# Loading the compression's weights one stage earlier, and spreading the row copies over the sparse attention

## The chip, the cores and the metric

The kernel runs on one core of one Trainium2 chip. The metric is the device time of one execution in microseconds; lower is better. TensorE multiplies matrices (PE; its weight loads are PEld), VectorE (DVE) and ScalarE (ACT) do elementwise work, GpSimd (POOL) a little of it, and SyncE (SP) issues most of the transfers. SP, ACT and POOL each have a DMA queue of their own (q1, q10 and q0 in the profile); all three are served by the same 16 DMA engines.

## The reference, cut to what matters

The program is one inference step of a two-layer decoder trunk: a prompt of 256 tokens and 8 samples of 8 new tokens each. Layer 0 is dilated attention beside a convolution module; layer 1 is a sparse attention with three branches (compressed, selected, sliding window). Of layer 1 this matters here:

```
def compress(x, pos, w1, b1, w2):          # once for keys, once for values
    blocks = concat(chunk[i], chunk[i+1]) + pos          # 32 rows, step 16
    h = silu(einsum('bnlgd,lde->bnge', blocks, w1) + b1)
    return einsum('bnge,ed->bngd', h, w2)

rows     = stack([kc, vc, ks, vs])         # new rows of this step
cs_full  = concat([cache_c_kv paged by page_table, rows])
win_full = concat([win_hist, stack([kw, vw])])
# outputs: rows of prompt and samples, and the last 512 rows of win_full for each
```

Each sample has 2048 past rows, in 16 pages of 128 rows; which page is read from `page_table`. The compression reads a page's raw keys and values, the selected branch its other two rows. `w1` is 2 x 32 x 128 x 128 floats (4 MB).

## The kernel before, in words

The program is a row of stages, each a block of code with a stream of instructions for every engine, and a barrier of all engines between one stage and the next. Engines wait for each other only on semaphores. The stages around the change:

- `block_even_out_odd_in`: the output projection of layer 0 (`out`), then the input projection of layer 1 (`proj`, from here on "the odd projection"). `proj` makes 11 groups of 512 output rows. Each group's weights come as four quarters of 1 MB on SP's queue into four buffers; a quarter's buffer is loaded again when PE has finished with it. ACT casts a quarter (`w_hi`, L352), DVE makes the remainder (`w_lo`, L414), PE multiplies (`zc`, L318 and L324). POOL's queue carries, after each group, one 4 MB piece of a cache copy from HBM to HBM (`send`, L1389), once the load of the gate (`mix<-z`, L1403), and at the end the store of the gate (L1405). SP stores the residual `xT` to `xt` after its last weights (L1334).
- `block_sample_c`: the sparse attention of the 8 samples. SP loads the page table (L1683), then for each sample 16 pages of raw rows (`raw`, 256 KB each, L1699) and 16 pages of the selected branch (`sel`, L1712). For each page SP first reads the page number from on-chip memory into a register (L1687). `raw` is one buffer in four pieces of four pages; a piece is loaded again when PE has turned its rows. POOL loads the tables of the bias (`bias_sc`, `gt`), fills the queries of sample 0, and issues the copies of rows to the outputs. ACT issues the compression's weights (`cmp_w`, `cmp_pos`, `cmp_b`, L1576 to L1582) and then evacuates.
- PE in this stage runs a software pipeline over samples (`body`): `turn_raw` transposes two pages, `taps` multiplies the turned rows with `w1`. `body(b)` does the attention of sample b, the second half of the compression of sample b+1, and, from its step 16 of 32 on, the first turns of sample b+2. `body(-1)` has no attention: steps 0 to 15 finish the turns of sample 0 and do its key taps, steps 16 to 31 turn the first rows of sample 1 between the value taps of sample 0. So `body(-1)` stops at its step 16 until the first piece of sample 1's raw rows is there.
- `pos_products` multiplies the positions with `w1` (64 small products), `sum_parts` adds them up to a bias that the first hidden layer needs.

SP's instructions run in order, and what SP does in this stage before it can issue sample 1's raw rows is written out as

```
load_raw(0, True)
for i in range(4): ...   # qs, then kn, ov, hs
load_rest(0, True)
load_raw(1)
```

Of the kernel before, what the change touches and what calls it, by code (L numbers as in the profile page):

```python
# [12 lines left out]
ALU = mybir.AluOpType  # L13
# [1282 lines left out]

def block_even_out_odd_in(nc, k):

    with k.scope():  # L1300
        mixed = Mix(k, "2")
        mix, gate = mixed.mix, mixed.gate
        xT = k.sb("xT2", [P, KT, T])
        gcol = k.sb("gcol2", [P, KT])
        wg, wgl = k.sb_and_lo("wg", [P, KT, P])
# [19 lines left out]
        with nc.Block() as block:  # L1325
            @block.sync
            def _(sp):
                view = lambda a: a.rearrange("(k p) t -> p k t", p=P)
# [10 lines left out]
                sp.wait_ge(xt_stored, 16)  # L1339
                sp.wait_ge(proj.z_stored, 16 * 12)  # L1340
                sp.wait_ge(proj.rows_stored, 32 * 4)
# [38 lines left out]
            @block.gpsimd  # L1380
            def _(pool):
                pool.memset(wg[:, :, :], 0.0).then_inc(wg_set, 1)
                pool.wait_ge(mixed.loaded[3], 32)
                pool.dma_start(xT[:, :, :], k.xt.rearrange("(k p) t -> p k t", p=P)).then_inc(x_in, 16)
                pieces = k.cache_pieces[15:23] + k.cache_pieces[40:46]
                link = Chain(pool, x.chain)

                def send(n):
                    pool.dma_start(*pieces[n]).then_inc(copied, 16)  # L1389

                for g in range(4):
# [15 lines left out]
                pool.wait_ge(copied, 16 * len(pieces))  # L1407

# [151 lines left out]
class Compress:  # L1560

    def __init__(self, k):
        self.k = k
        self.w1, self.w2, self.pos, self.b1, self.bias, self.nbias = (
            k.sb(name, shape, lasting=True) for name, shape in (
                ("cmp_w1", [P, 2, CB, HD]), ("cmp_w2", [P, 2, HD]), ("cmp_pos", [P, 2 * CB]), ("cmp_b1", [P, 2]),
                ("cmp_bias", [P, 2]), ("cmp_nbias", [P, 2])))
        self.parts = k.sb("cmp_parts", [P, 2 * HD])  # L1570
        self.zero = k.sb("cmp_zero", [P, 2 * HD])
        self.loaded, self.small, self.zeroed, self.done, self.parts_ready, self.summed, self.ready = (
            k.sem(n) for n in ("cmp_in", "cmp_small_in", "cmp_zeroed", "cmp_pos_done", "cmp_parts_ready", "cmp_summed", "cmp_bias_ready"))

    def load(self, act):
        act.dma_start(self.pos[:, :], self.k.cmp_pos).then_inc(self.small, 16)  # L1576
        act.dma_start(self.b1[:, :], self.k.cmp_b1).then_inc(self.small, 16)
        for i in range(2):
            for part in range(2):
                l = slice(part * CB // 2, (part + 1) * CB // 2)  # L1580
                act.dma_start(self.w1[:, i, l, :], self.k.cmp_w1[i][l].rearrange("l d e -> d l e")).then_inc(self.loaded, 16)
        act.dma_start(self.w2[:, :, :], self.k.cmp_w2.rearrange("a e d -> e a d")).then_inc(self.small, 16)  # L1582

    def pos_products(self, pe, bank, i):

        if i == 0:
            pe.wait_ge(self.small, 48)
            pe.wait_ge(self.zeroed, 1)
            pe.matmul(bank[:, 0:2 * HD], self.zero[:, 0:P], self.zero[:, :], start=True, stop=True)
        for l in range(CB):  # L1590
            o = 32 * (l % 4)
            ins = pe.matmul(bank[o:o + 1, i * HD:(i + 1) * HD], self.pos[:, i * CB + l:i * CB + l + 1], self.w1[:, i, l, :],
                            start=(l < 4), stop=(l >= CB - 4))
        ins.then_inc(self.done, 1)

    def sum_parts(self, pe, bank):
        pe.wait_ge(self.parts_ready, 1)
        for i in range(2):
            ins = pe.matmul(bank[:, 2 * HD + i:2 * HD + i + 1], self.parts[:, i * HD:(i + 1) * HD], self.k.ones[:, 0:1], start=True, stop=True)
        ins.then_inc(self.summed, 1)  # L1600

    def dve(self, dve, bank):
        dve.wait_ge(self.done, 2)
        dve.tensor_copy(self.parts[:, :], bank[:, 0:2 * HD]).then_inc(self.parts_ready, 1)
        dve.wait_ge(self.summed, 1)
        link = Chain(dve, self.ready)
        link(dve.tensor_tensor(self.bias[:, :], bank[:, 2 * HD:2 * HD + 2], self.b1[:, :], ALU.add))
        link(dve.tensor_scalar(self.nbias[:, :], self.bias[:, :], -1.0, None, ALU.mult))

def block_sample_c(nc, k):
# [3 lines left out]
    with k.scope():  # L1615
        k.compress = cmp = Compress(k)
        ptab = k.sb("ptab", [1, NB * NPG], mybir.dt.int32)
# [40 lines left out]
        pt_in = k.sem("pt_in")  # L1658
# [21 lines left out]
        with nc.Block() as block:  # L1680
            @block.sync
            def _(sp):
                sp.dma_start(ptab[:, :], dram_ap(k.page_table, 0, [(NB * NPG, 1), (1, NB * NPG)])).then_inc(pt_in, 16)  # L1683
                sp.wait_ge(pt_in, 16)

                def pages_of(b):
                    return [sp.value_load(ptab[0:1, bass.ds(b * NPG + pg, 1)], min_val=0, max_val=k.cache_c_kv.shape[0] - 1)  # L1687
                            for pg in range(NPG)]

                def load_raw(b, first=False):  # L1690
                    page = pages_of(b)
                    for pg in range(NPG):
                        n = pg * NPIECE // NPG
                        if not first and pg % (NPG // NPIECE) == 0:
                            sp.wait_ge(raw_turned, b * NR + (NRK - NR + 2 * n + 2))
                            settle(sp, k)

                        rows = k.cache_c_kv[bass.ds(page[pg], 1)].rearrange("a (n l) c g d -> (a l) n (c g d)", l=CS)[:, :, 0:2 * CKV]
                        sp.dma_start(raw[:, pg, :], rows).then_inc(raw_in[n], 16)  # L1699
# [36 lines left out]
            def _(pool):  # L1736
# [22 lines left out]
                n = 0  # L1759
                for dst, c0, c1 in ((k.out_rows_p, 0, 4 * CKV), (k.out_win_p, 4 * CKV, 6 * CKV)):  # L1760
                    pool.dma_start(dst.rearrange("t c g d -> t (c g d)"), k.kv2[0:NP, c0:c1]).then_inc(rows_out, 16)
                    n += 1
                pool.dma_start(k.out_rows_s.rearrange("b t c g d -> (b t) (c g d)"), k.kv2[NP:T, 0:4 * CKV]).then_inc(rows_out, 16)
                n += 1
                for b in range(NB):
                    pool.dma_start(k.out_win_s[b, 0:WIN - NQ].rearrange("t c g d -> t (c g d)"), k.cache_c_win[b, NQ:WIN].rearrange("t c g d -> t (c g d)")).then_inc(rows_out, 16)
                    pool.dma_start(k.out_win_s[b, WIN - NQ:WIN].rearrange("t c g d -> t (c g d)"), k.kv2[NP + b * NQ:NP + (b + 1) * NQ, 4 * CKV:]).then_inc(rows_out, 16)
                    n += 2
                with pool.Fori(1, NB) as b:
                    fill_q(b)  # L1770
                pool.wait_ge(rows_out, 16 * n)
# [17 lines left out]
            def _(act):  # L1789
                cmp.load(act)  # L1790

# [55 lines left out]
            def _(pe):  # L1847
# [143 lines left out]
                def body(b, attend=True, make=True, ahead=True, first=False):  # L1991
                    for n in range(STEPS):
                        if make:
# [5 lines left out]
                            if not attend and n == 8:  # L1999
                                cmp.pos_products(pe, ob, 1)  # L2000
                            if not attend and n == 12:
# [14 lines left out]

                for j in range(NRK):
# [376 lines left out]
class Kit:  # L2394
# [15 lines left out]

    def sb_and_lo(self, name, shape):
# [130 lines left out]
```

## Time and profile before

| | |
|---|---|
| median of three runs | 2876.9 us (2875.43 to 2877.23) |
| the profiled execution's own time | 2879.94 us |
| its span, first to last instruction | 2878.1 us |
| mean granted TensorE clock | 0.896 of 2.4 GHz |
| the odd projection's last product | 1921 us from the span's start |
| first instructions of the sparse attention of the samples | 1945.0 us |
| its end (the store of its output) | 2533 us |

Times in the views are counted from the start of the span. The profiled execution is 3.0 us above the median and 1.8 us above its own span; a change in a stage is a change of all three by the same amount.

### The profile page before, as it was taken

To read this page: it belongs to the slowest core of one execution; us is meant where nothing else is said; L and a number is where in the kernel's file an instruction comes from. 1 tells how busy PE (TensorE), PEld (TensorE's weight loads), DVE (VectorE), ACT (ScalarE), POOL (GpSimd) and SP (SyncE) were. 2 spreads that over 40 slices of the span, in tenths; PEclk is the share of its full clock that TensorE was granted. 3 is DMA by queue.
4 is the path that set the end of the run, shared out by engine and by line. 5 is a ranking of instruction groups with operands and counts; after the bars stand their busy time and mean duration, and the time that the engine had idled before them with its cause. 6 is when DMAs were issued, how large, how long until landed. Compare 5 with 4: busy or idle time off the path is not lost. (4 is left out here: it accounts for less than half of the span.)

```text
span 2878.1 us, 49626 instructions
## 1 busy us (share of the span) xinstructions
PE 2411.9 (84%) x18820; PEld 2140.5 (74%) x18820; DVE 1270.3 (44%) x2311; ACT 752.2 (26%) x1100; POOL 184.1 (6%) x326
## 2 busy tenths in 40 slices
PE   6799999899689559995679999962599999877597
PEld 3799999888589436664569999962488888666496
DVE  2436699635166123332344536720043334426545
ACT  1333333333043112220133322211133333213321
POOL 1000100000000310000023200002100000000000
PEclk8899999999899779995579999985799999958799
DMA  4787888865678799994388688888745454225382
GB/s 133 271 325 282 298 322 323 289 205 165 239 249 315 248 374 380 405 349 152 97 287 283 223 306 315 323 307 164 258 147 161 146 187 149 74 67 183 135 321 76
DMA packets 260279, 686.04 MB, mean 238 GB/s; under 512 B 31814, under 2 KB 83823, under 8 KB 256557
## 3 DMA queue, kind: packets, MB, share of 16 engines
q1 hardware_dynamic: 213790, 415.74, 41.9%
q0 software_dynamic: 17312, 229.03, 21.9%
q10 hardware_dynamic: 29072, 39.82, 4.2%
q8 instruction: 71, 1.16, 0.2%
q14 instruction: 34, 0.28, 0.0%
HBM read 631.32 MB, written 250.80 MB: 306 GB/s over the span
## 5 line engine op out<-in xcount | busy, mean ns | idle before, releaser
L414 DVE TENSOR_TENSOR w_lo<-w,w_hi 128x2048 fp32r<-128x2048 f32 x180 | 415.1, 2313 | 346.5 <-ACT w_hi L352 333.4
L352 ACT CAST w_hi<-w 128x2048 fp32r<-128x2048 f32 x176 | 335.4, 1908 | 791.8 <-DMA w<-in_w_in_even 220.9
L318 PE MATMUL zb<-xh,w_hi 128*128 128x320 f32 x1664 | 496.8, 312 | 33.0 <-ACT w_hi L348 20.6
L318 PE MATMUL zb<-xT_lo,w_hi 128*128 128x320 f32 x1664 | 494.4, 311 | 0.0
L318 PEld LDWEIGHTS zb<-xh,w_hi 128*128 128x128 f32 x1664 | 316.9, 190 | 34.5 <-ACT w_hi L348 20.7
L318 PEld LDWEIGHTS zb<-xT_lo,w_hi 128*128 128x128 f32 x1664 | 316.4, 190 | 0.2
L324 PE MATMUL zb<-xh,w_lo 128*128 128x320 f32 x1664 | 267.5, 313 | 15.5 <-DVE w_lo L414 15.5
L324 PEld LDWEIGHTS zb<-xh,w_lo 128*128 128x128 f32 x1664 | 254.0, 192 | 16.6 <-DVE w_lo L414 16.6
L1865 PE MATMUL hb<-xtc,cmp_w 128*128 128x254 f32 x1024 | 252.8, 384 | 0.0
L318 PE MATMUL zc<-xh,w_hi 128*128 128x320 f32 x704 | 208.9, 311 | 8.0 <-ACT w_hi L352 6.6
L318 PE MATMUL zc<-xl,w_hi 128*128 128x320 f32 x704 | 208.3, 310 | 0.0
L1865 PEld LDWEIGHTS hb<-xtc,cmp_w 128*128 128x128 f32 x1024 | 182.9, 192 | 21.8 <-issue 4.5
L970 PE MATMUL kps<-ident,ka 128*128 128x128 f32 x832 | 141.0, 296 | 43.1 <-DMA ka<-in_cache_a_kv 41.8
L1855 PE MATMUL xrb<-ident,raw 128*128 128x128 f32 x512 | 82.2, 286 | 110.9 <-DMA raw<-in_cache_c_kv 104.4
L1855 PEld LDWEIGHTS xrb<-ident,raw 128*128 128x128 f32 x512 | 65.8, 147 | 127.9 <-DMA raw<-in_cache_c_kv 64.7
L970 PEld LDWEIGHTS kps<-ident,ka 128*128 128x128 f32 x832 | 92.2, 146 | 87.8 <-DMA ka<-in_cache_a_kv 44.1
L1797 ACT COPY xtc<-xrb 128x512 f32<-128x512 f32 x128 | 74.9, 585 | 288.9 <-PE xrb L1855 288.9
L947 DVE COPY ktt<-kps 128x512 f32<-128x512 f32 x104 | 71.9, 692 | 167.0 <-PE kps L970 167.0
L318 PEld LDWEIGHTS zc<-xh,w_hi 128*128 128x128 f32 x704 | 133.1, 189 | 8.7 <-issue 5.4
L318 PEld LDWEIGHTS zc<-xl,w_hi 128*128 128x128 f32 x704 | 133.0, 189 | 0.1
L947 ACT COPY ktt<-kps 128x512 f32<-128x512 f32 x104 | 60.9, 586 | 226.5 <-PE kps L970 226.5
L324 PE MATMUL zc<-xh,w_lo 128*128 128x320 f32 x704 | 111.9, 312 | 3.3 <-DVE w_lo L414 3.3
(372 smaller groups left out, 3424.5 us busy)
## 6 DMA issues: line engine op xcount, KB each, us to landing
out<-in_cache_a_kv POOLq DMA_DIRECT2D x32, 4080.0 KB, 16.5
w<-in_w_in_even SPq DMA_DIRECT2D x104, 1024.0 KB, 7.5
ka<-in_cache_a_kv SPq DMA_DIRECT2D x24, 2048.0 KB, 13.1
va<-in_cache_a_kv SPq DMA_DIRECT2D x24, 2048.0 KB, 15.0
w<-in_w_in_odd SPq DMA_DIRECT2D x44, 1024.0 KB, 10.1
raw<-in_cache_c_kv SPq DMA_DIRECT2D x128, 256.0 KB, 4.0
sel<-in_cache_c_kv SPq DMA_DIRECT2D x128, 256.0 KB, 5.5
out<-in_cache_a_kv POOLq DMA_DIRECT2D x8, 4032.0 KB, 21.6
```

The source lines that it names most:

```text
L318: ins = pe.matmul(self.banks[c][:, 0:T], self.hi[:, q % 2, j, c * P:(c + 1) * P], x[:, q * self.kq + j, :], start=(q == 0 and j == 0 and m ...
L324: ins = pe.matmul(self.banks[c][:, 0:T], self.lo[:, q, j, c * P:(c + 1) * P], self.xh[:, q * self.kq + j, :], start=False, stop=(q == self ...
L352: act.copy(self.hi[:, q % 2, :, :], self.wt[:, q % 4, :, :]).then_inc(self.hi_ready, 1)
L414: dve.tensor_tensor(self.lo[:, q, :, :], self.wt[:, q, :, :], self.hi[:, q % 2, :, :], ALU.subtract).then_inc(self.lo_ready, 1)
L947: copy(ktt[:, q % 2, :], kps[q % 2][:, :]).then_inc(sem, 1)
L970: ins = pe.transpose(kps[q % 2][:, j * P:(j + 1) * P], kt[g][:, r, h * HD:(h + 1) * HD], k.ident[:, :])
L1797: act.copy(xt[:, 2 * kv:2 * kv + 2, :, chunks:chunks + 2 * n].rearrange("p g l (u n) -> p u (g l) n", n=n), xr[:, :].rearrange("p (u c n) ...
L1855: ins = pe.transpose(xr[:, (2 * u + g) * P:(2 * u + g + 1) * P], raw[:, 2 * (j % NRK) + u, (2 * kv + g) * P:(2 * kv + g + 1) * P], k.ident ...
L1865: ins = pe.matmul(hb[i][:, 0:CG * NCS], cmp.w1[:, i, l, :], xt[:, 2 * i:2 * i + 2, l % CS, l // CS:l // CS + NCS], start=(l == 0), stop=(l ...
```

## The change

Three things are done.

1. The compression's weights, positions, biases and the page table are loaded in the stage before, on POOL's queue. Their tiles lie at the addresses of `xT2` and `wg`, which are used up by then (`sb_shared` gives an address back at once, so that later tiles may lie there too). For that `xT` is stored earlier, on POOL's queue too, right after the sums of squares; the small tensors follow it, and the four parts of `w1` (1 MB each, in rows of 512 bytes) go ahead of the pieces 5 to 8.
2. SP begins the sparse attention with the raw rows: it reads a page's number and issues that page's load, sixteen times. The products with the positions stand first on PE.
3. POOL's copies of rows to the outputs go later. Those of a sample's window follow its query fill, inside POOL's loop over samples; the others follow that loop.

```
@@ block_even_out_odd_in
+        xT, wg = k.sb_shared(("xT2", [P, KT, T], F32), ("wg", [P, KT, P], F32))
+        k.compress = cmp = Compress(k)
...
             def _(sp):
...
                 proj.sync(sp)
-                sp.dma_start(view(k.xt), xT[:, :, :]).then_inc(xt_stored, 16)
...
             def _(pool):
...
+                pool.dma_start(k.xt.rearrange("(k p) t -> p k t", p=P), xT[:, :, :]).then_inc(xt_stored, 16)
+                cmp.load_small(pool)
                 for n in range(3, len(pieces)):
                     pool.wait_ge(proj.tile_done, 4 * (n - 3) + 8)
+                    if n == 5:
+                        pool.wait_ge(xt_stored, 16)
+                        pool.wait_ge(x.summed, 1)
+                        pool.wait_ge(x.ready, KT)
+                        pool.wait_ge(gl_done, 1)
+                    if 5 <= n < 9:
+                        cmp.load(pool, n - 5)
                     send(n)
@@ Compress
+    def load_small(self, eng):
+        eng.dma_start(self.ptab[:, :], dram_ap(self.k.page_table, 0, [(NB * NPG, 1), (1, NB * NPG)])).then_inc(self.small, 16)
...
+    def load(self, eng, part):
+        i, l = part // 2, slice(part % 2 * CB // 2, (part % 2 + 1) * CB // 2)
+        eng.dma_start(self.w1[:, i, l, :], self.k.cmp_w1[i][l].rearrange("l d e -> d l e")).then_inc(self.loaded, 16)
@@ block_sample_c
             def _(sp):
-                sp.dma_start(ptab[:, :], dram_ap(k.page_table, 0, [(NB * NPG, 1), (1, NB * NPG)])).then_inc(pt_in, 16)
-                sp.wait_ge(pt_in, 16)
...
                 def load_raw(b, first=False):
-                    page = pages_of(b)
+                    page = None if first else pages_of(b)
...
             def _(pool):
...
                 fill_q(0)
-                for b in range(NB):
-                    pool.dma_start(k.out_win_s[b, 0:WIN - NQ]...
+                with pool.Fori(1, NB) as b:
+                    fill_q(b)
+                    rows_of(b)
+                rows_of(0)
...
             def _(act):
-                cmp.load(act)
...
             def _(pe):
...
+                for i in range(2):
+                    cmp.pos_products(pe, ob, i)
                 for j in range(NRK):
                     turn_raw(0, j)
-                pe.wait_ge(cmp.loaded, 64)
-                cmp.pos_products(pe, ob, 0)
                 body(-1, attend=False)
```

On POOL in the odd projection, after the last sum of squares (`sq`, `sum`), there stood before: the pieces of the cache copy (`out<-in_cache_a_kv`) and the load of the gate (`mix<-z`).

```order
L1274 TENSOR_TENSOR sum<-sum,sq 128x320
L1389 DMA out<-in_cache_a_kv 64x16320 x3
L1403 DMA mix<-z 128x16x320
L1389 DMA out<-in_cache_a_kv 64x16320 x8
L1405 DMA gate<-mix 128x16x320
```

And now, at the same place:

```order
+L1454 DMA xt<-xT 128x16x320
+L1311 DMA ptab<-in_page_table 1x16x8
+L1312 DMA cmp_pos<-in_cmp_pos 128x64
+L1313 DMA cmp_b<-in_cmp_b 128x2
+L1314 DMA cmp_w<-in_cmp_w 128x2x128
+L1446 DMA out<-in_cache_a_kv 64x16320 x2
+L1318 DMA cmp_w<-in_cmp_w 128x16x128
+L1446 DMA out<-in_cache_a_kv 64x16320
+L1469 DMA mix<-z 128x16x320
+L1318 DMA cmp_w<-in_cmp_w 128x16x128
+L1446 DMA out<-in_cache_a_kv 64x16320
+L1318 DMA cmp_w<-in_cmp_w 128x16x128
```

The store of `xT` and the small tensors stand ahead of the first two of these pieces, and a part of `w1` stands ahead of each of the next pieces (the fourth follows in the same way); the load of the gate keeps its place behind piece 5.

On SP at the start of the sparse attention there stood before the load of the page table, then sixteen times the read of a page's number, then sixteen loads (the first of each are shown):

```order
-L1683 DMA ptab<-in_page_table 1x128
-L1687 TENSOR_LOAD ptab
-L1687 ISA x2
...
-L1699 ISA
-L1699 DMA raw<-in_cache_c_kv 128x1x512
...
-L1720 DMA qsc<-z 128x4x64 x4
```

And now read and load alternate from the stage's first instruction on, sixteen times:

```order
L1700 TENSOR_LOAD ptab
L1700 ISA x2
L1714 ISA
L1714 DMA raw<-in_cache_c_kv 128x1x512
...
L1735 DMA qsc<-z 128x4x64 x4
```

On PE at the same place there stood the turns of the first eight pairs of pages (`xrb`), half of the products with the positions, and the first taps (`hb`), with the other half of the products further on:

```order
L1855 MATMUL xrb<-ident,raw 128x128 x32
L1589 MATMUL ob<-cmp_zero 128x256
L1592 MATMUL ob<-cmp_w,cmp_pos 1x128 x32
L1865 MATMUL hb<-xtc,cmp_w 128x254 x2
```

And now all products with the positions come first:

```order
L1333 MATMUL ob<-cmp_zero 128x256
L1336 MATMUL ob<-cmp_w,cmp_pos 1x128 x64
L1870 MATMUL xrb<-ident,raw 128x128 x32
L1880 MATMUL hb<-xtc,cmp_w 128x254 x2
```

## Rows read from the trace of the kernel before

**Rows 1.** The page: PE's busy share in 40 slices of 72 us.

```profile
PE   6799999899689559995679999962599999877597
```

**Rows 2.** Stretches around the stage's start: length, busy of PE, PEld, DVE, ACT, POOL; clock; DMA.

```profile
1919.10:1945.00 25.90, 1.52 (x12) 1.26 (x12) 0.22 (x1) 1.54 (x3) 1.67 (x2) 0.64 0.85 313
1945.00:1985.40 40.40, 0.00 (x0) 0.00 (x0) 0.00 (x0) 1.37 (x4) 19.71 (x40) 0.50 1.02 168
1985.40:2007.60 22.20, 13.14 (x98) 8.41 (x98) 0.00 (x0) 4.68 (x8) 0.00 (x0) 0.50 0.61 174
2007.60:2028.90 21.30, 21.22 (x172) 18.11 (x168) 1.74 (x5) 5.15 (x9) 2.94 (x8) 0.99 0.73 256
2028.90:2063.70 34.80, 0.00 (x0) 0.00 (x0) 2.22 (x2) 0.00 (x0) 7.27 (x15) 0.55 1.00 344
...
2212.00:2270.00 58.00, 57.61 (x449) 46.88 (x448) 22.77 (x53) 18.16 (x38) 0.56 (x3) 1.00 0.49 163
```

**Rows 3.** Waits of PE from 1921 to 2064: total us, times, longest.

```profile
PE xrb L1855 <- DMA raw<-in_cache_c_kv: 104.4, 3, 64.5
```

**Rows 4.** Timeline of SP's queue from 1940 to 2130: start, length, count.

```profile
1945.03 0.27 SPq L1683 DMA_DIRECT2D ptab<-in_page_table  x1
1955.97 31.82 SPq L1699 DMA_DIRECT2D raw<-in_cache_c_kv  x16
1987.85 9.05 SPq L1720 DMA_DIRECT2D qsc<-z  x4
...
1999.65 1.08 SPq L1724 DMA_DIRECT2D hs<-in_c_hsum  x1
2009.73 0.37 SPq L1705 DMA_DIRECT2D win<-in_cache_c_win  x1
...
2019.87 0.29 SPq L1716 DMA_DIRECT2D vnc<-kv  x1
2029.45 87.68 SPq L1699 DMA_DIRECT2D raw<-in_cache_c_kv  x32
```

**Rows 5.** The same queue, from 1955 to 1962.7 only.

```profile
1955.97 6.57 SPq L1699 DMA_DIRECT2D raw<-in_cache_c_kv  x9
```

**Rows 6.** Landing of raw pages issued in 1940 to 1990, 2029 to 2045, 2063 to 2545.

```profile
DMA to landing us min/median/max: 19.4/27.0/31.9
...
DMA to landing us min/median/max: 29.9/30.5/31.9
...
DMA to landing us min/median/max: 3.3/3.9/5.4
```

**Rows 7.** DMA from 2026 to 2064: a queue's MB and share; issues, median landing.

```profile
q0 software_dynamic: 1008, 10.23, 76.6%
...
out<-in_cache_c_win POOLq DMA_DIRECT2D x8, 1008.0 KB, 17.3
```

**Rows 8.** Timeline of PE from 1984 to 2010, one turn of two pages.

```profile
1995.07 1.12 PE L1855 MATMUL xrb<-ident,raw 128*128 128x128 f32 x4 [0.68 <-ACT xtc L1797]
```

**Rows 9.** DMA from 1948 to 1956, ACT's queue (the parts of w1).

```profile
q10 hardware_dynamic: 707, 1.42, 83.7%
```

**Rows 10.** Stretches of the odd projection, one group each from 1708 on.

```profile
1597.00:1612.30 15.30, 15.18 (x102) 15.02 (x103) 6.18 (x6) 4.24 (x3) 0.06 (x1) 1.00 0.44 138
...
1708.00:1737.00 29.00, 25.59 (x164) 25.06 (x162) 11.84 (x9) 4.13 (x3) 1.77 (x3) 0.94 0.88 309
1737.00:1774.00 37.00, 30.49 (x196) 30.26 (x197) 22.81 (x23) 13.78 (x6) 0.45 (x2) 0.95 0.80 296
1774.00:1802.20 28.20, 28.20 (x194) 28.20 (x194) 22.45 (x21) 7.64 (x4) 0.54 (x2) 1.00 0.88 320
```

**Rows 11.** Waits of all engines from 1708 to 1775.

```profile
ACT w_hi L352 <- DMA w<-in_w_in_odd: 27.0, 3, 15.9
...
PE zc L318 <- ACT w_hi L352: 6.6, 2, 3.5
```

**Rows 12.** Waits of SP's queue from 2063 to 2545.

```profile
SPq L139 <- PE xrb L1855: 83.6, 19, 13.9
```

More of the change, by code:

```diff
@@ L1294, in make_lo, with __init__, start, pos_products @@
                                  ALU.mult, ALU.subtract).then_inc(self.ready, 1)
+class Compress:
+    def __init__(self, k):
+        self.k = k
+        self.w1, self.w2, self.pos, self.b1, self.bias, self.nbias = (
+            k.sb(name, shape, lasting=True) for name, shape in (
+                ("cmp_w1", [P, 2, CB, HD]), ("cmp_w2", [P, 2, HD]), ("cmp_pos", [P, 2 * CB]), ("cmp_b1", [P, 2]),
+                ("cmp_bias", [P, 2]), ("cmp_nbias", [P, 2])))
+        self.ptab = k.sb("ptab", [1, NB * NPG], mybir.dt.int32, lasting=True)
+        self.loaded, self.small = (k.sem(n) for n in ("cmp_in", "cmp_small_in"))
+    def load_small(self, eng):
+        eng.dma_start(self.ptab[:, :], dram_ap(self.k.page_table, 0, [(NB * NPG, 1), (1, NB * NPG)])).then_inc(self.small, 16)
+        eng.dma_start(self.pos[:, :], self.k.cmp_pos).then_inc(self.small, 16)
+        eng.dma_start(self.b1[:, :], self.k.cmp_b1).then_inc(self.small, 16)
+        eng.dma_start(self.w2[:, :, :], self.k.cmp_w2.rearrange("a e d -> e a d")).then_inc(self.small, 16)
+    def load(self, eng, part):
+        i, l = part // 2, slice(part % 2 * CB // 2, (part % 2 + 1) * CB // 2)
+        eng.dma_start(self.w1[:, i, l, :], self.k.cmp_w1[i][l].rearrange("l d e -> d l e")).then_inc(self.loaded, 16)
+    def start(self):
+        k = self.k
+        self.parts = k.sb("cmp_parts", [P, 2 * HD])
+        self.zero = k.sb("cmp_zero", [P, 2 * HD])
+        self.zeroed, self.done, self.parts_ready, self.summed, self.ready = (
+            k.sem(n) for n in ("cmp_zeroed", "cmp_pos_done", "cmp_parts_ready", "cmp_summed", "cmp_bias_ready"))
+    def pos_products(self, pe, bank, i):
+        if i == 0:
+            pe.wait_ge(self.zeroed, 1)
+            pe.matmul(bank[:, 0:2 * HD], self.zero[:, 0:P], self.zero[:, :], start=True, stop=True)
+        for l in range(CB):
+            o = 32 * (l % 4)
+            ins = pe.matmul(bank[o:o + 1, i * HD:(i + 1) * HD], self.pos[:, i * CB + l:i * CB + l + 1], self.w1[:, i, l, :],
+                            start=(l < 4), stop=(l >= CB - 4))
+        ins.then_inc(self.done, 1)
+    def sum_parts(self, pe, bank):
+        pe.wait_ge(self.parts_ready, 1)
+        for i in range(2):
+            ins = pe.matmul(bank[:, 2 * HD + i:2 * HD + i + 1], self.parts[:, i * HD:(i + 1) * HD], self.k.ones[:, 0:1], start=True, stop=True)
+        ins.then_inc(self.summed, 1)
+    def dve(self, dve, bank):
+        dve.wait_ge(self.done, 2)
+        dve.tensor_copy(self.parts[:, :], bank[:, 0:2 * HD]).then_inc(self.parts_ready, 1)
+        dve.wait_ge(self.summed, 1)
+        link = Chain(dve, self.ready)
+        link(dve.tensor_tensor(self.bias[:, :], bank[:, 2 * HD:2 * HD + 2], self.b1[:, :], ALU.add))
+        link(dve.tensor_scalar(self.nbias[:, :], self.bias[:, :], -1.0, None, ALU.mult))
@@ L1407, in _ @@
                 pool.wait_ge(copied, 16 * len(pieces))
+                pool.wait_ge(cmp.small, 64)
+                pool.wait_ge(cmp.loaded, 64)
             @block.tensor
@@ L1557 @@
 NSC = O_C + NCS
[L1560 to L1608, printed above, removed]
@@ L1611, in block_sample_c @@
 def block_sample_c(nc, k):
     with k.scope():
-        k.compress = cmp = Compress(k)
-        ptab = k.sb("ptab", [1, NB * NPG], mybir.dt.int32)
+        cmp = k.compress
+        cmp.start()
         raw = k.sb("raw", [P, NPG, 2 * CKV])
@@ L1682, in _, with page_of @@
             def _(sp):
[L1683 to L1684 removed]
+                def page_of(b, pg):
+                    return sp.value_load(cmp.ptab[0:1, bass.ds(b * NPG + pg, 1)], min_val=0, max_val=k.cache_c_kv.shape[0] - 1)
                 def pages_of(b):
[L1687 to L1688 removed]
+                    return [page_of(b, pg) for pg in range(NPG)]
                 def load_raw(b, first=False):
[L1691 removed]
+                    page = None if first else pages_of(b)
                     for pg in range(NPG):
@@ L1696, in load_raw @@
                             settle(sp, k)
-                        rows = k.cache_c_kv[bass.ds(page[pg], 1)].rearrange("a (n l) c g d -> (a l) n (c g d)", l=CS)[:, :, 0:2 * CKV]
+                        rows = k.cache_c_kv[bass.ds(page_of(b, pg) if first else page[pg], 1)].rearrange("a (n l) c g d -> (a l) n (c g d)", l=CS)[:, :, 0:2 * CKV]
                         sp.dma_start(raw[:, pg, :], rows).then_inc(raw_in[n], 16)
@@ L1998, in body @@
                                 turn_raw(b + 2, n // 2 - NRK)
-                            if not attend and n == 8:
-                                cmp.pos_products(pe, ob, 1)
-                            if not attend and n == 12:
+                            if not attend and n == 2:
                                 cmp.sum_parts(pe, ob)
@@ L2015, in body @@
                             turn(b, TURNS_AT[n])
+                for i in range(2):
+                    cmp.pos_products(pe, ob, i)
                 for j in range(NRK):
                     turn_raw(0, j)
-                pe.wait_ge(cmp.loaded, 64)
-                cmp.pos_products(pe, ob, 0)
                 body(-1, attend=False)
@@ L2409, in sb, with sb_shared @@
         return self.stacks[0 if lasting else -1].enter_context(self.nc.sbuf_tensor(name, shape, dt))
+    def sb_shared(self, *named):
+        with ExitStack() as stack:
+            return [stack.enter_context(self.nc.sbuf_tensor(name, shape, dt)) for name, shape, dt in named]
     def sb_and_lo(self, name, shape):
```

21 lines of the change are left out of this document (7 added, 14 removed).

## The prediction

> **What bounds the kernel now.** I began with the page's slices [rows 1]. PE is busy nine tenths of most of them, but slices 28 and 29 (1943 to 2087 us) show 2 and 5: the longest hole of the program, at the start of the samples' sparse attention, where the change works. Cut into stretches [rows 2], it is two holes. From 1945.0 to 1985.4 PE does nothing; from 2028.9 to 2063.7 again nothing; between them lies work of body(-1). Both end with the same releaser [rows 3]: PE waits for raw pages, 104.4 us in three waits (the longest, 64.5, counts from PE's last work before the barrier). After that it is PE that binds: 57.6 of 58.0 us in a stretch as long as one sample, the last of [rows 2]. So what counts is when PE passes the second hole; whatever makes that earlier moves all later work by as much.
>
> Who is late at the holes is read from SP's queue [rows 4]. The stage begins at 1945.03 with the page table. The first raw load goes out at 1955.97, after 10.9 us of waiting for the table and reading sixteen numbers. Nine loads go out at 0.73 us each [rows 5], then the queue backs up, and sixteen take 31.8 us. Their landing takes 27 us where an undisturbed page takes 3.9 [rows 6], since all 16 DMA engines are taken: 1.02 of their time, at only 168 GB/s [rows 2]. Most of that is w1 on ACT's queue [rows 9]. Then SP goes on in order: queries and constants until 2000.7, sixteen numbers until 2009.7, window and selected pages until 2020.2, sixteen numbers until 2029.45, and only then sample 1's raw rows. These land after another 30 us [rows 6], because POOL's row copies have 76.6% of the DMA engines' time from 2026 on [rows 7].
>
> **The second hole after the change.** It ends when sample 1's fourth raw page has landed. Counted from the stage's start:
>
> - Sixteen times a number and a load. A number costs 0.56 us (2000.73 to 2009.73 for sixteen [rows 4]), a load 0.73: 20.7 us. DMA no longer has w1 to serve, so I let the queue not back up.
> - Queries and constants: 12.9 us before [rows 4], with the backlog of raw rows ahead of them. The bound below is 6, eight issues at the 0.73 us of a load that does not back up; I take 10, in the middle.
> - Sixteen numbers 9.0; window, selected pages and new values 10.4; sixteen numbers 9.3 [rows 4]. Nothing in the change touches these.
> - Three more issues, 2.2 us, and a landing of 3.9, the later samples' [rows 6]. The row copies are gone from here, and selected pages issued before have 9.3 us to land.
>
> The sum is 65.5 us. Before, PE went on at 2063.7, which is 118.7 after the start. The difference is **53.2 us**.
>
> Is PE itself there by then? Its last raw page of sample 0 is issued 20 us after the start and lands by 24 to 28; two turns of 1.8 us remain (1.12 busy and 0.68 idle [rows 8]); steps 0 to 15 took 21.3 us [rows 2], with half of the position products in them, which now lie in the first hole. At half clock for a few us (0.50 granted, that is 1.2 GHz, after the first hole [rows 2]) this may be 3 more. So PE is at step 16 after 49 to 56 us and still waits 10 to 16 for SP. The hole shrinks from 34.8 us but does not close; SP's chain ends it, and DMA speed at the start matters only if it is worse by over 10 us.
>
> **What is added in the stage before.** Four parts of w1 go through POOL's queue beside the odd projection's weights, and that stage has little DMA left: 0.88 of the time in an undisturbed group of 28.2 us, the last of [rows 10], so 3.4 us free. A part's price comes from the queue of before: 1.42 MB at 83.7% of 8 us [rows 9] is 4.7 us per MB, so 4.9 for a part of 1.05. That is 1.5 us too much in such a group. Two of the parts fall into the stretch 1708 to 1774, where PE already waits: the load of the gate and the pieces delay the weights, ACT waits 27.0 us for them, PE 6.6 for ACT [rows 11], and the clock's share falls to 0.94 and 0.95 [rows 10]. There I count half of the two parts, 5 us at most. The bounds are 0 (the weights' four buffers take it all) and 20 (all four parts exposed). I take **5**, nearer to the lower end, because PE is busy for the whole of the group beside 0.88 of DMA time. If it is more, PE stands before ACT's next cast, and DVE and POOL's next piece stand behind PE.
>
> The Trainium skill speaks on this price too. Its page "DMA: Bandwidth & Descriptors", section Specifications, puts line rate at transfers of at least 512 bytes and the fabric's ceiling at 435 GB/s; w1 comes in rows of 512 bytes. By that a part would take 2.4 us (an estimate from that page), no group would overrun, and the time would be 2824. The row of before disagrees: with 83.7% of the engines w1 got 212 GB/s per full engine set.
>
> The earlier store of xT (2.6 MB) meets a stretch with DMA at 0.44, the first of [rows 10], so nearly 9 us of DMA time are free before the next piece; nothing, at worst inside the 20 above. POOL's new waits at piece 5 are for work done groups earlier; behind them stand the piece and the gate's load, which waits longer anyhow. The barrier's own 24 us (1921 to 1945) keep their cause, the last piece and the gate's store ahead of the last rows; nothing changes there.
>
> **The copies inside the sample loop.** One window copy of 1 MB per sample costs 2.9 us of DMA time (76.6% of 38 us for 10.23 MB [rows 7]), and DMA is half idle there (0.49 [rows 2]). SP has 12 us per sample in which it waits for PE (83.6 over seven [rows 12]), so a load delayed by a copy is still early. Cost 0; without that cover up to 2.9 per sample, 20 in all. What POOL does after its loop has the last sample's time as cover.
>
> **Sum.** From the profiled execution's 2879.94: minus 53.2, plus 5, is 2831.7; the median of the runs lies 3.0 lower, so **2829**.
>
> **Rivals.**
>
> - *The odd projection becomes DMA-bound.* For it: 0.88, and PE's waits between 1708 and 1774. Against it: the four buffers, and that groups with the same 0.88 show no wait. Price 20 instead of 5: 2844. Chance 0.15.
> - *SP's chain stays late*, since sixteen raw loads back up behind the bias tables, which stay on POOL's queue; the change then does only its second half. SP would issue sample 1 near 2029 as before and its piece would land in 6 us instead of 34: a gain of 28, minus 5: 2854. Against it: of the 1.02 in the first hole most was w1. Chance 0.08.
> - *Everything at its better end*: constants in 6 us, landing 3.3, no price in the odd projection: 57.8 us gained, 2819. Chance 0.12.
> - *Slower than before.* The copies in the loop, with their large packets, hold selected pages back past what PE needs, in each sample. It decides only from 7 us per sample on (seven times 7 is the 48 of the forecast), against a price of 2.9 and 12 us of slack. 2880 and more. Chance 0.02.
>
> The forecast itself, 2822 to 2837, has 0.61; some 0.02 remain for no visible change.
>
> **How the numbers follow.** A measurement of this kernel tells 0.2%, 5.8 us, from no change. All but the last case are far below: faster 0.96, same 0.02, slower 0.02. The range leaves out these two and the late chain, 12 in 100, and some of what spread the cases at its ends have of their own: 2815 to 2852.
>
> **What would show it.** In the changed profile, SP's first raw load stands within 1 us of the stage's start and the sixteenth some 21 us later; PE's first turn comes some 10 us after the start; the second hole is 8 to 18 us long and ends 63 to 70 us after the start, its releaser still the raw rows; their landing is near 4 us. In the odd projection the groups with a part are 0 to 5 us longer, all of it before w_hi. The forecast is wrong if SP's sixteen loads still take 30 us, if those four groups grow by 20 in all, or if a sample takes over 60 us.

## The result and the profile after

The changed kernel took 2841.06 us, the median of four runs (2838.27 to 2852.85), against 2876.16 us (2862.84 to 2877.23) for the kernel before on the same chip: a ratio of 0.9896 (95% interval 0.9856 to 0.9936). It is faster by 35 us, and 12 us above the forecast of 2829. The profiled execution is the longest of the four, 2852.85 us, with a span of 2851.3 us, 26.8 us below that of before. How that comes about, stage by stage (after minus before, from starts and ends in the two traces): up to the fourth piece of GpSimd's cache copy in the odd projection (n = 3 in the code, which counts from 0) -1.4; from there to its last product +12.4; the barrier behind it +1.2; the sparse attention of the samples -42.4; the prompt's attention +3.4. The sum is -26.8. The prediction had two terms, +5 and -53.2. Both point the right way, and both are 7 to 11 us too good.

**The sparse attention's start.** The page's PE slices first:

```profile
PE   6799999989879559995669997992899999876597
```

Where [rows 1] had a 2 and a 5 side by side there is one 2 now, from 1925 to 1996 us (the barrier and the first hole), and an 8 behind it. The stretches that answer to [rows 2], with raw(0) and raw(1) for the raw rows of samples 0 and 1: the position products and a wait, the turns of raw(0), steps 0 to 15, the second hole, and one sample's length:

```profile
1957.30:1970.30 13.00, 5.89 (x131) 3.97 (x131) 0.42 (x1) 0.00 (x0) 12.86 (x27) 0.76 0.86 158
1970.30:2000.40 30.10, 8.87 (x33) 5.72 (x33) 0.00 (x0) 4.69 (x8) 6.96 (x14) 0.50 0.82 141
2000.40:2021.30 20.90, 20.90 (x104) 18.09 (x104) 1.02 (x3) 5.15 (x9) 0.56 (x3) 0.88 0.65 240
2021.30:2033.80 12.50, 0.43 (x3) 0.08 (x2) 2.52 (x3) 0.01 (x1) 0.00 (x0) 0.68 0.44 133
2182.00:2240.00 58.00, 57.60 (x450) 46.87 (x449) 22.78 (x53) 18.12 (x38) 1.60 (x5) 1.00 0.55 181
```

PE's waits from 1921 to 2064, the line that answers to [rows 3]:

```profile
PE xrb L1870 <- DMA raw<-in_cache_c_kv: 36.0, 4, 13.6
```

104.4 us have become 36.0. The releaser is the same. SP's queue, which [rows 4] showed of before:

```profile
1958.26 20.90 SPq L1714 DMA_DIRECT2D raw<-in_cache_c_kv  x16
1979.20 14.63 SPq L1735 DMA_DIRECT2D qsc<-z  x4
1993.87 2.60 SPq L1737 DMA_DIRECT2D knc<-z  x2
...
1996.95 0.68 SPq L1739 DMA_DIRECT2D hs<-in_c_hsum  x1
2006.60 0.37 SPq L1720 DMA_DIRECT2D win<-in_cache_c_win  x1
2007.17 9.98 SPq L1727 DMA_DIRECT2D sel<-in_cache_c_kv  x16
...
2017.62 0.30 SPq L1731 DMA_DIRECT2D vnc<-kv  x1
2027.21 11.68 SPq L1714 DMA_DIRECT2D raw<-in_cache_c_kv  x16
```

Read it as a sum, from the stage's start at 1957.28: raw(0) with its numbers to 21.9, queries and constants 18.4, numbers 9.0, window and selected pages 11.3, numbers 9.3, then 6.5 to PE's first turn of raw(1) at 76.5. The row that stands out is the queries': four loads in 14.63 us, where sixteen raw loads with their numbers took 20.90. DMA from 1957 to 1982 (a queue's packets, MB, share; issues and their median landing) shows what stands there:

```profile
q1 hardware_dynamic: 1566, 2.87, 70.0%
q0 software_dynamic: 1026, 1.00, 24.3%
...
raw<-in_cache_c_kv SPq DMA_DIRECT2D x16, 256.0 KB, 8.6
bias_sc<-tab_hc POOLq DMA_DIRECT2D x16, 64.2 KB, 6.5
```

raw(0) lands in 8.6 us, not 27.0 [rows 6], but not in 3.9 either: GpSimd's queue (q0) is loading the bias tables.

**The odd projection.** Four groups of it, from one of GpSimd's pieces to the next, n = 5 to n = 9; the third answers to 1737 to 1774 in [rows 10]:

```profile
1675.50:1713.50 38.00, 34.67 (x237) 34.41 (x236) 18.20 (x13) 13.11 (x8) 2.85 (x4) 1.00 0.91 312
1713.50:1735.30 21.80, 21.80 (x150) 21.55 (x149) 6.15 (x9) 4.10 (x3) 1.64 (x2) 1.00 1.09 407
1735.30:1786.20 50.90, 31.37 (x197) 31.14 (x196) 22.81 (x21) 11.81 (x5) 1.74 (x3) 0.80 0.69 240
1786.20:1813.20 27.00, 27.00 (x187) 27.00 (x186) 21.15 (x20) 7.65 (x4) 0.56 (x2) 1.00 1.01 363
```

And the waits in the middle two, beside [rows 11]:

```profile
ACT w_hi L352 <- DMA w<-in_w_in_odd: 28.3, 3, 19.4
...
PE zc L318 <- ACT w_hi L352: 19.5, 1, 19.5
```

In the group with part 1 and piece 6, DMA is taken whole (1.09) and PE does not stop once. The price falls due one group later: PE waits 19.5 us for a cast that waits for a quarter of w, and the group takes 50.9 us in place of 37.0. The last group, with part 3, is as short as ever, at a DMA share of 1.01.

**The copies in the loop.** The wait that gives SP its slack, from 2034 to 2515 [rows 12]:

```profile
SPq L139 <- PE xrb L1870: 78.1, 19, 9.0
```

78.1 us are left of 83.6; PE's busy time in the last of the stretches above is 57.60 of 58.00, and GpSimd's copies of a sample's keys follow each other by 58.4 to 58.8 us in both traces.

### The profile page after: what moved, and what is told of

It reads as the page before. It is cut to its first block and busy times, and to the rows that moved or that the text cites. A ratio compares the mean times of both kernels' runs of the same rounds, so it can differ in the third digit from the quotient of the medians.

```text
span 2851.3 us, 49669 instructions
## 1 busy us (share of the span) xinstructions
PE 2405.1 (84%) x18820; PEld 2134.2 (75%) x18820; DVE 1270.0 (45%) x2311; ACT 751.5 (26%) x1096; POOL 193.2 (7%) x335
## 3 DMA queue, kind: packets, MB, share of 16 engines
q1 hardware_dynamic: 211724, 413.12, 42.4%
## 5 line engine op out<-in xcount | busy, mean ns | idle before, releaser
L318 PE MATMUL zb<-xh,w_hi 128*128 128x320 f32 x1664 | 496.4, 311 | 34.4 <-ACT w_hi L348 20.6
L318 PEld LDWEIGHTS zb<-xh,w_hi 128*128 128x128 f32 x1664 | 316.9, 190 | 35.9 <-ACT w_hi L348 20.7
L318 PE MATMUL zc<-xh,w_hi 128*128 128x320 f32 x704 | 209.7, 312 | 20.9 <-ACT w_hi L352 19.5
L970 PEld LDWEIGHTS kps<-ident,ka 128*128 128x128 f32 x832 | 91.6, 145 | 89.4 <-DMA ka<-in_cache_a_kv 46.1
## 6 DMA issues: line engine op xcount, KB each, us to landing
ka<-in_cache_a_kv SPq DMA_DIRECT2D x24, 2048.0 KB, 13.5
```

Source lines behind the costliest of these rows:

```text
L318: ins = pe.matmul(self.banks[c][:, 0:T], self.hi[:, q % 2, j, c * P:(c + 1) * P], x[:, q * self.kq + j, :], start=(q == 0 and j == 0 and m ...
L970: ins = pe.transpose(kps[q % 2][:, j * P:(j + 1) * P], kt[g][:, r, h * HD:(h + 1) * HD], k.ident[:, :])
```

## The experiments

Ten kernels ran in three jobs, each beside the kernel before (medians 2870.82, 2876.42 and 2871.12). The table has the times, and three readings of each profile: the third group of the odd projection (n = 7 to n = 8), TensorE's first turn of raw(1), and GpSimd's second copy of keys (knb), from which on every sample takes the same time. The last two count from the sparse attention's start.

| kernel | median us (lowest to highest, runs) | ratio to before, 95% | group | raw(1) | knb |
|---|---|---|---|---|---|
| before | 2876.16 (2862.84 to 2877.23, 4) | | 37.0 | 118.7 | 165.4 |
| the change | 2841.06 (2838.27 to 2852.85, 4) | 0.9896 (0.9856 to 0.9936) | 50.9 | 76.5 | 123.1 |
| after_again | 2836.60 (2829.66 to 2846.56, 4) | 0.9866 (0.9815 to 0.9917) | 48.7 | 74.5 | 119.8 |
| parts_later | 2827.88 (2825.88 to 2832.84, 4) | 0.9842 (0.9799 to 0.9885) | 35.4 | 75.7 | 121.2 |
| bias_late | 2839.68 (2833.21 to 2844.31, 4) | 0.9873 (0.9830 to 0.9916) | 45.3 | 74.9 | 121.0 |
| copies_only | 2840.53 (2840.04 to 2847.61, 4) | 0.9891 (0.9847 to 0.9935) | 34.8 | 89.4 | 134.7 |
| weights_only | 2871.81 (2860.89 to 2880.61, 10) | 0.9989 (0.9967 to 1.0012) | 45.4 | 100.0 | 146.9 |
| part2_later | 2843.24 (2832.45 to 2847.15, 4) | 0.9879 (0.9852 to 0.9906) | 46.8 | 71.7 | 117.5 |
| raw_first | 2833.80 (2829.45 to 2844.23, 4) | 0.9837 (0.9813 to 0.9861) | 50.7 | 63.2 | 106.9 |
| all_three | 2822.38 (2814.00 to 2826.11, 4) | 0.9793 (0.9764 to 0.9821) | 37.9 | 49.8 | 113.2 |
| two_later | 2835.40 (2823.15 to 2837.08, 5) | 0.9870 (0.9811 to 0.9929) | 34.5 | 74.2 | 119.7 |
| bias_between | 2814.82 (2798.41 to 2821.10, 4) | 0.9776 (0.9709 to 0.9843) | 35.7 | 50.1 | 98.3 |

The times of one kernel lie up to 23 us apart here, those of the kernel before 31 (2856.41 to 2887.88), so the columns on the right tell more than a single time does; they come from one profile of each kernel.

**after_again**: the changed kernel, unedited.

> The changed kernel itself, profiled a second time. If the 50.8 us of the odd projection's stretch with parts 1 and 2 (before 37.0) is the order of the transfers there, the stretch takes 49 to 52 us again and the profiled time is about 2850 us. If it was chance of one execution, it takes 37 to 42 us and the profiled time is 2838 to 2842 us.

The same group in its profile:

```profile
1732.40:1781.10 48.70, 30.15 (x196) 29.92 (x196) 22.71 (x21) 11.73 (x5) 1.64 (x2) 0.82 0.71 250
```

48.7 us, a little under the forecast band, and 11.7 above before; its own time, 2842.86, lies between the two forecasts. The stall isn't chance. Over the five profiles with all four parts in their places (the change twice, bias_late, weights_only, raw_first) the group took 45.3 to 50.9 us, and from n = 3 to the last product 316.8 to 321.3 us, mean 319.0; before and copies_only took 308.4 and 306.3. The parts' price is 11.6 us.

**parts_later**

```
-                    if n == 5:
+                    if n == 9:
                         pool.wait_ge(xt_stored, 16)
...
-                    if 5 <= n < 9:
-                        cmp.load(pool, n - 5)
+                    if 9 <= n < 13:
+                        cmp.load(pool, n - 9)
```

> The changed kernel with the four parts of w1 sent four pieces later (n = 9 to 12 in place of 5 to 8). If parts 1 and 2 beside the gate's load starve the w quarters, the wait of 19.5 us on w_hi is gone, the stretch that took 50.8 us takes about 37 us, and the kernel is 8 to 14 us faster than the changed kernel's 2852.9 us profile, 2838 to 2844 us. Rival: four parts cost the same wherever they stand, a stall of 10 to 14 us appears at the later pieces, and the time is within 3 us of the changed kernel. If the stall was chance, the two agree too, but neither shows it.

```profile
1732.30:1767.70 35.40, 30.54 (x196) 30.31 (x197) 22.92 (x23) 13.79 (x6) 0.55 (x2) 0.95 0.83 309
```

The stall is gone and comes back nowhere: from n = 3 to the last product it is 306.8 us. The same bytes, four pieces later, cost nothing, although DMA's share is 0.98 to 0.99 from 1823 to 1883 us there. The median lies 8.7 us below after_again, in the same job; the profiled time, 2828.79, is 24 us under that of the changed kernel and below the forecast band, so it holds other differences too. The edit also moves GpSimd's four waits; two_later, below, leaves them where they are and loses the stall as well.

**part2_later** and **two_later** take the parts away from piece 7, and from pieces 6 and 7:

```
-                    if 5 <= n < 9:
-                        cmp.load(pool, n - 5)
+                    if n in (5, 6, 8, 9):
+                        cmp.load(pool, (5, 6, 8, 9).index(n))
```

> The changed kernel with the parts of w1 at n = 5, 6, 8 and 9 in place of 5 to 8: parts 0 and 1 stay (part 1 behind the gate's load), piece 7 goes without a part. If part 2 with piece 7 is what cuts the w quarters off, the wait of 18.5 to 19.5 us on w_hi falls to 2 to 6 us and the odd projection takes 302 to 305 us in place of 314.7. If part 1 beside the gate's load has already put the w quarters behind, it stays at 311 to 316 us. A part at n = 9 costs nothing in either.

> The changed kernel with the parts of w1 at n = 5, 8, 9 and 10: parts 0 and 3 keep their places, pieces 6 and 7 go without a part. If a part beside the gate's load is what puts the w quarters behind, the odd projection takes 302 to 305 us as with all four parts later, the single waits on w_hi are under 4 us, and the kernel is 8 to 12 us faster than the changed one (2828 to 2834 us). If any part at n = 5 to 8 costs its bytes, half of the price stays: 308 to 311 us.

(two_later has 5, 8, 9, 10 in those two lines.) The group in part2_later, and then in two_later:

```profile
1732.80:1779.60 46.80, 34.25 (x204) 34.02 (x205) 24.08 (x24) 13.89 (x6) 1.75 (x3) 0.85 0.69 241
```

```profile
1730.40:1764.90 34.50, 30.18 (x204) 29.95 (x205) 24.12 (x24) 13.14 (x6) 1.73 (x3) 1.00 0.84 304
```

Without a part ahead of piece 7 the price stays (46.8; 317.1 us in all, or 313.0 on the expectation's count, which begins some 4 us later); without one ahead of piece 6 as well it is away (34.5; 305.9). So one part behind the gate's load of 2.6 MB and ahead of piece 6 is enough (piece 5 had one ahead in both runs), and those ahead of pieces 5 and 8 cost nothing. The part ahead of piece 7 adds little beside it (2 us to the mean); what it would cost without a part ahead of piece 6 was not run. The six profiles with a part ahead of piece 6 took 316.8 to 321.3 us, the six without 305.9 to 308.4. two_later's median, 2835.40, misses its band and doesn't show the gain against the changed kernel; its trace does, and what holds the other runs up no trace shows.

How it comes about is seen in who had the DMA engines ahead of the stall: the first 21 us of the group, in the change (1735 to 1756) and then before (1737 to 1758).

```profile
q0 software_dynamic: 356, 5.49, 71.3%
q1 hardware_dynamic: 549, 1.09, 16.3%
```

```profile
q0 software_dynamic: 80, 4.18, 52.3%
q1 hardware_dynamic: 1657, 3.30, 41.2%
```

GpSimd's queue moved 5.49 MB in place of 4.18, and SP's queue, with the quarters of w, 1.09 in place of 3.30. That is more than the part's own megabyte. GpSimd's packets are long (5.49 MB in 356, 15 KB each on average; before 52 KB), those of w are 2 KB, and while both queues have work they go one for one: from 1747 to 1751 in the change 29 packets of GpSimd's (1.89 MB) and 31 of w's (0.06 MB), before, from 1745 to 1749, 20 (1.31 MB) and 24 (0.05 MB). The Trainium skill, page "DMA: Bandwidth & Descriptors", section "Queues, rings and completion order", says that an engine goes round its queues one packet at a time. The counts agree with it, if the profile's packets are the page's. So w gets few bytes here for as long as the copy's long packets run, and most of its bytes in the gap between one piece and the next. From 1732 to 1740 GpSimd's queue moved 0.07 MB and w's 2.02 before; in the change GpSimd's queue, with piece 6 late behind the part, still moved 1.45 MB, and w's 0.52. In two_later the gap is there again (1724 to 1733: 0.00 and 2.42 MB), and the first 20.6 us of its group are like those of before:

```profile
q0 software_dynamic: 80, 4.18, 53.9%
q1 hardware_dynamic: 1485, 2.95, 39.1%
```

This is read from one trace each; no run takes the long packets away.

**copies_only** is the kernel before with GpSimd's part of the sparse attention as in the change; **weights_only** is the change with GpSimd's part as before.

> The kernel before with one part of the change: the rows' copies go inside the loop over the samples and behind it; weights and page table stay where they were. If the copies of 10.2 MB are what held up the second raw load (landings of 27.0 and 30.5 us), landings fall to 4 to 8 us, the wait of 64.5 us falls to about 10 us, and the kernel takes 2842 to 2852 us, 25 to 35 us less than before. If the weights standing ahead were the main hold, it gains under 10 us. If the copies cost their time again inside the loop, the period of a sample rises over 58.6 us and the time is within 10 us of before.

> The changed kernel with the rows' copies back in one block behind the first fill of the queries, so that only the weights and the page table move. The first two runs of parts put the copies' share at 30 us and the odd projection's price at 12 us. If the second raw load meets the copies as before, it takes 34 us from its first issue to the last landing, the second hole ends about 104 us behind the stage's start (before 118.7), and with the odd projection's 12 us more the time is within 8 us of before. Rival: the copies too start 15 us earlier, are done earlier and leave the second raw load free; then the hole ends at 80 to 90 us and the kernel gains 16 us or more.

PE's waits at the stage's start, in copies_only and then in weights_only:

```profile
PE xrb L1857 <- DMA raw<-in_cache_c_kv: 75.5, 3, 63.2
```

```profile
PE xrb L1869 <- DMA raw<-in_cache_c_kv: 59.6, 4, 36.0
```

In copies_only the first hole stays (63.2 of the 75.5) and the second nearly closes (7.2 of them). The 64.5 us that the expectation names were the first hole's wait, the wrong one; the second's, 34.9 before, is what fell: raw(1) lands in a median of 4.7 us and its first turn comes at 89.4 in place of 118.7. The median is 30.3 us below before, where after_again in the same job has 34.2: nearly all of the change's gain. In weights_only the first hole closes and the second stays, 36.0 us. Its SP queue shows where the row copies meet it:

```profile
1994.22 29.42 SPq L1727 DMA_DIRECT2D sel<-in_cache_c_kv  x16
...
2037.61 52.84 SPq L1714 DMA_DIRECT2D raw<-in_cache_c_kv  x26
```

The copies start earlier, as the rival had it, but then hold the selected pages (29.42 us where the change takes 9.98), and raw(1) goes out late. raw(1) is turned at 100.0, 18.7 us earlier than before; the odd projection takes 10 us of that back, and the time, 0.9989 (0.9967 to 1.0012), can't be told from before. The forecast of hole and time held, its reason only in part: raw(1) itself landed in 5.1 us.

**bias_late**

```
                 pool.memset(rank[:, 0, :], 1.0e30).then_inc(zeroed, 1)
+                pool.wait_ge(raw_turned, NRK)
```

> The changed kernel, with GpSimd's loads of the bias tables in the sparse attention put behind a wait for TensorE's first eight turns. If the 1.3 MB of these tables hold up raw(0) and what stands behind it, raw(0)'s packets fall from 140 to 229 ns towards 84 ns, the queries and constants take 9 to 11 us of SP's time in place of 18.4, the first turns come 10 to 15 us earlier, TensorE resumes after its second hole 65 to 69 us behind the stage's start in place of 76.5, and the kernel is 7 to 10 us faster. Rival: the queries' 18.4 us is the price of their own small packets, SP's chain stays where it is, and the time is within 3 us of the changed kernel although the first turns come earlier.

```profile
1955.66 20.61 SPq L1714 DMA_DIRECT2D raw<-in_cache_c_kv  x16
1976.31 2.24 SPq L1735 DMA_DIRECT2D qsc<-z  x4
...
1980.57 0.72 SPq L1739 DMA_DIRECT2D hs<-in_c_hsum  x1
...
1990.85 17.48 SPq L1727 DMA_DIRECT2D sel<-in_cache_c_kv  x16
2008.38 4.10 SPq L1730 DMA_DIRECT2D vnc<-kv  x1
...
2022.21 11.68 SPq L1714 DMA_DIRECT2D raw<-in_cache_c_kv  x16
```

PE's waits there:

```profile
PE xrb L1871 <- DMA raw<-in_cache_c_kv: 35.1, 5, 24.0
```

Half of the theory holds. Queries and constants fall from 18.4 to 5.0 us, raw(0) lands in 3.4 us, and the turns of raw(0) are over 13.5 us earlier. But the tables then stand against the selected pages, which grow from 9.98 to 17.48 us, and the new values (vnc) from 0.7 to 4.4: SP sends raw(1) 67.5 us after the start in place of 69.9, and PE waits 24.0 us for it. The cost was moved, not removed, and the forecast of 7 to 10 us failed: the median is 3.1 us above after_again's in the same job.

**raw_first**

```
-                load_rest(0, True)
                 load_raw(1)
+                load_rest(0, True)
```

> The changed kernel, with SP's order at the start of the sparse attention turned round: raw(1) first, then win, sel and vnc of sample 0. If SP's place in line is what holds the second raw load, its first issue comes about 50 us behind the stage's start in place of 69, TensorE resumes at 65 to 67 us in place of 76 (the hole of 12 us shrinks to 1 to 3), and the kernel is 8 to 12 us faster than the changed one. Rival: sel and vnc of sample 0, now 20 us later, become the next hold, or raw(1) has to wait for raw(0)'s turns, and the time is within 3 us of the changed kernel.

```profile
2011.71 16.06 SPq L1714 DMA_DIRECT2D raw<-in_cache_c_kv  x16
2036.62 0.38 SPq L1720 DMA_DIRECT2D win<-in_cache_c_win  x1
```

PE's waits from 1935 to 2070:

```profile
PE xrb L1870 <- DMA raw<-in_cache_c_kv: 21.3, 3, 12.8
```

All three are for raw(0): raw(1) goes out 48.4 us after the start, the second hole is gone, and its first turn comes at 63.2, 11 to 13 us earlier; the keys' copy (106.9) comes 13 to 16 us earlier, so nothing of it is lost to the selected pages. SP's place in line was the hold. The times say less: the median, 2833.80, is 3 and 7 us below the two of the changed kernel, from other jobs, where 8 to 12 were forecast, and the intervals meet. The profiled execution has the odd projection's stall near its worst (50.7).

**all_three** joins parts_later, raw_first and bias tables that wait for raw(1)'s landing; **bias_between** is the same, with tables that wait for raw(0)'s only:

```
-                pool.wait_ge(raw_in[NPIECE - 1], 128)
+                pool.wait_ge(raw_in[NPIECE - 1], 64)
```

> Parts of w1 at n = 9 to 12, raw(1) ahead of sample 0's rest on SP, and the bias tables put behind raw(1)'s landing on GpSimd. If the three costs are separate, the odd projection takes 302 us, the queries and constants 5 us of SP's time in place of 16.7 to 18.4, raw(1) is issued from 36 us behind the stage's start, TensorE resumes at 52 to 56 us in place of 76, and the kernel takes 2802 to 2812 us, 24 us or more less than the changed one. Rival: the bias tables' 17 us of issues and 1.3 MB then fall on sel and the first sample's softmax, and a wait of VectorE gives 10 us or more of it back.

> The kernel with the three edits (parts of w1 at n = 9 to 12, raw(1) first on SP, bias tables held back), but the bias tables wait only for raw(0) to have landed, not raw(1). If the 15 us that TensorE then waited on knb and on the keys' copy came from bias tables that were issued at 55 us behind the stage's start, tables issued at 22 to 26 us are in by 50 us, both waits are gone, raw(1) lands 2 to 6 us later for sharing the queues, and the kernel takes 2806 to 2816 us, 8 to 15 us less than with the tables behind raw(1). Rival: tables and raw(1) now collide as tables and raw(0) did, TensorE resumes 10 us later, and nothing is gained.

PE's waits at the start in all_three, then VectorE's:

```profile
PE xsb L1923 <- DVE kttc L1797: 8.4, 1, 8.4
PE mb L1982 <- POOL knbc L1771: 5.9, 1, 5.9
```

```profile
DVE kttc L1797 <- DMA gt<-gates_s: 26.7, 1, 26.7
```

Both holes are closed (first turn of raw(1) at 49.8), and the rival's waits appear: GpSimd copies the keys behind 19 us of issues of tables and gates, VectorE waits for the gates among them. 14 us go there, and the time misses its band. In bias_between both are gone; the second hole's stretch and the next 58 us there:

```profile
2004.60:2007.40 2.80, 0.40 (x2) 0.00 (x0) 0.00 (x0) 0.00 (x0) 0.00 (x0) 1.00 1.06 276
2007.40:2065.40 58.00, 57.67 (x402) 47.49 (x403) 19.75 (x43) 18.37 (x38) 1.62 (x5) 0.97 0.62 203
```

PE stops for 2.8 us at a DMA share of 1.06 and then runs full; the second keys' copy comes at 98.3 in place of 113.2. At 2814.82 us, in its band, it has the lowest median here; that it is faster than all_three (7.6 us by the medians, 8 to 15 forecast) the times don't show, since the intervals overlap. Its interval, 0.9709 to 0.9843, still meets after_again's too, but the median lies 22 us below.

## Why the prediction was right, and where its terms were off

The time, 2841.06, lies inside the stated range of 2815 to 2852 and outside the forecast itself, 2822 to 2837. The two main terms missed in the same direction, so nothing cancelled; it was the width of the range that held. The prediction also took 5.8 us for what runs can tell apart, from three that agreed; thirteen runs of the kernel before, in one job, lie between 2860.29 and 2885.80.

**That SP's chain ends the second hole: right.** The releaser, the order and the length of the hole (12.5 us, 10 to 16 forecast) came as said, and raw_first shows it by experiment. The time at which it ends did not: 76.5, where 63 to 70 was the sign.

**The end of that hole: 65.5 us forecast, 76.5 measured.** Term by term: raw(0) with its numbers 20.7 against 21.9, the first of them 1.0 us after the start; numbers 9.0 and 9.0; window, selected pages and new values 10.4 against 11.3; numbers 9.3 and 9.3; the last issues and the landing 6.1 against 6.5. The mis-sized term is queries and constants, taken at 10 in the middle of 6 and 12.9, measured at 18.4: above its own upper bound. I had let the queue not back up once w1 was gone; the tables on GpSimd's queue backed it up again. bias_late shows the term without them: 5.0. The step that misled was "most of that is w1": [rows 9] cover the 8 us ahead of the first raw load. While the raw loads were being issued, 1956 to 1988 before, w1 had 48.3% of the engines' time, SP's own queue 38.7% and GpSimd's tables 20.7%.

**The rival of SP's late chain** had the right culprit, the bias tables, and the wrong victim: the raw loads' issues did not slow (20.9 us), the loads behind them did.

**PE itself: step 16 at 49 to 56 us forecast, 64.0 measured**, for the same reason: the turns of raw(0) waited for its landings. It stayed hidden behind SP's chain; bias_late has 50.5.

**The odd projection: 5 us, "half of the two parts", measured 11.6** over five profiles, 12.4 in the profiled one, within the bounds of 0 and 20. The stretch was right, 1708 to 1774; what failed is the pricing by bytes. One part between the gate's load and piece 6 is enough for all of it, those ahead of pieces 5 and 8 cost nothing, and one group grew by 13.9 us where 0 to 5 for each was the sign. The price of a part's bytes was off too: 4.9 us came from w1 on ACT's queue, in packets of 2 KB beside the tables.
**The copies in the loop at 0: right**, by SP's slack and the unchanged 58.4 us. **The two halves of the change** were not told apart by the prediction. The copies' move carries nearly all of the gain; the weights' move, worth 13 to 15 us more at raw(1)'s first turn, loses about as much in the odd projection. With the parts four pieces later it is a gain: parts_later's four runs lie at 2825.88 to 2832.84, those of copies_only in the same job at 2840.04 to 2847.61.

Against the profiled execution the sum was 2831.7 and the time 2852.85, 21 us more: 10.8 from the samples' sparse attention, 7.4 from the odd projection, 3 from the stages that the prediction left alone. The other three runs of the changed kernel were 12 to 15 us shorter than the profiled one; where, no trace of them shows.

## What to carry to other kernels

When a load is moved into a stage whose DMA is nearly full, ask which transfer stands beside it, not how many bytes fit: the same parts cost 11.6 us when one stood behind a large load and nothing four pieces later, and the wait showed one group behind the one that caused it. When a backlog is taken off a queue, look for the next-largest tenant of the engines at that moment before pricing the queue as free. And where one queue serves several stages in a fixed order, its order is the cheapest thing to change: two exchanged lines brought raw(1)'s first turn forward by 11 to 13 us, about what moving 4 MB did, and took nothing back in the stage before.

## What the runs showed of the hardware beyond that

- One megabyte of tables on a second queue made the first queue's packets slower, not only fewer. While raw(0) is loaded, 0.760 of 16 engines over 20 us (1959 to 1979) for 1397 packets is 174 ns each in the change; 0.604 over 20 us (1956.3 to 1976.3) for 2062 is 94 ns in bias_late, at the same mean size of 1.83 KB. Why a packet takes that long beside the tables stays open.
- Kernels whose instructions are the same up to there reached the odd projection's n = 3 between 1602.0 and 1618.1 us of their profiles. That is nearly as much as one kernel's times differ. The two earliest (1602.0 and 1604.5) had a granted clock of 0.91 from 1100 to 1400 us, the others 0.85 to 0.88; why it differs stays open.
- The last sample's 58.5 us, the same instructions in all, had a granted clock of 0.91 in three of nine profiles and 0.74 to 0.79 in six, and its end came about 4 us sooner in the three: as much as some of the effects above.
